# Two transformer blocks on one core: memory attention interleaved with its query projections, squared-relu fronts reordered, first value chunks 512 columns wide

## The reference

```python
def memory_cross_attention(h, mem_n, w_q, w_kv, w_o):       # first block, both layers
    q = (h @ w_q).reshape(B_, S_, MEM_HEADS, MEM_HEAD_DIM)   # 4 heads of 256
    kv = (mem_n @ w_kv).reshape(B_, M, 2, MEM_HEADS, MEM_HEAD_DIM)
    s = jnp.einsum('bshd,bmhd->bhsm', q, kv[:, :, 0]).astype(jnp.float32) * MEM_HEAD_DIM ** -0.5
    p = jax.nn.softmax(s, axis=-1).astype(h.dtype)
    o = jnp.einsum('bhsm,bmhd->bshd', p, kv[:, :, 1]).reshape(B_, S_, D_MODEL)
    return o @ w_o

def squared_relu_mlp(h, w1, w2):                             # first block, both layers; 4096 hidden
    a = jax.nn.relu(h @ w1)
    return (a * a) @ w2

# first block, layer 1: band attention; second block, layer 0: stick-breaking attention
qkv = (h @ w_qkv).reshape(B_, S_, 3, ATT_HEADS, ATT_HEAD_DIM)   # 16 heads of 64
```

## Time and profile before

| | |
|---|---|
| median of three runs | 1807.8 us |
| the profiled execution | 1808.25 us |
| its span on the core | 1806.3 us |
| TensorE busy | 1772.4 us, 98% |
| VectorE busy | 1160.9 us, 64% |
| ScalarE busy | 868.8 us, 48% |
| GpSimd busy | 62.1 us, 3% |
| HBM traffic | 318.08 MB, mean 176 GB/s |

### The profile page before, as it was taken

One profiled execution on the slowest core, in us unless ns is written; L12 is line 12 of the kernel. 1 busy time (PEld: TensorE's weight loads), 2 busy tenths in 40 slices (PEclk: granted clock), 3 DMA queues, 4 the chain that ended last, 5 costly groups with the idle time before them and its releaser, 6 DMA issues.

```text
span 1806.3 us, 25833 instructions
## 1 busy us (share of the span) xinstructions
PE 1772.4 (98%) x10482; PEld 1547.4 (86%) x10482; DVE 1160.9 (64%) x1166; ACT 868.8 (48%) x1060; POOL 62.1 (3%) x102
## 2 busy tenths in 40 slices
PE   9999999999999999999999999999999999999998
PEld 7889988888988878888888899888888888788887
DVE  6665465557456465556666755667676666876665
ACT  7535455556455454555433466533353334553343
POOL 1000000000120000000000100000000000110000
PEclk9999999999999999999999999999999999999999
DMA  9526356556546345554556553565555555336552
GB/s 310 183 70 221 106 187 202 194 186 189 164 160 229 105 162 202 197 196 155 184 189 205 169 163 117 176 208 178 194 175 186 193 194 186 118 117 210 187 184 93
DMA packets 217157, 318.08 MB, mean 176 GB/s; under 512 B 5585, under 2 KB 179809, under 8 KB 217074
## 3 DMA queue, kind: packets, MB, share of 16 engines
q1 hardware_dynamic: 212274, 300.96, 50.2%
q0 software_dynamic: 4800, 15.94, 2.8%
HBM read 315.83 MB, written 1.05 MB: 175 GB/s over the span
## 4 chain that ended last, share of the span: by engine, by line
PE 93%; DVE 4%; ACT 2%; issue 0%; DMA 0%; SPq 0%; ACTq 0%; DVEq 0%
PE Y L1824 29%; PE C L1747 22%; PE C L1751 12%; PE Y L1780 9%; PE C L1780 5%; PE C L1792 4%; PE Y L1714 3%; DVE xn L1178 1%; DVE w_lo L1137 1%; ACT xn L669 1%; PE C L2023 1%; PE C L1996 1%; PE C L1878 1%; PE Y L2043 1%; PE C L2317 1%; PE C L2035 1%
## 5 line engine op out<-in xcount | busy, mean ns | idle before, releaser
L1137 DVE TENSOR_TENSOR w_lo<-raw,w_hi 128x2048 fp32r<-128x2048 f32 x282 | 645.7, 2291 | 321.0 <-ACT w_hi L654 320.5
L654 ACT ACTIVATE w_hi<-raw 128x2048 fp32r<-128x2048 f32 x282 | 538.2, 1910 | 247.2 <-PE Y L1824 163.9
L1747 PE MATMUL C<-at_hl,w_hi 128*128 128x512 f32 x1440 | 342.8, 390 | 0.0
L1747 PEld LDWEIGHTS C<-at_hl,w_hi 128*128 128x128 f32 x1440 | 267.9, 188 | 54.1
L1824 PE MATMUL Y<-w_hi,hid_h 128*128 128x512 f32 x696 | 216.7, 392 | 0.0
L1824 PE MATMUL Y<-w_lo,hid_h 128*128 128x512 f32 x696 | 215.0, 390 | 0.0
L1824 PE MATMUL Y<-w_hi,hid_l 128*128 128x512 f32 x696 | 214.6, 390 | 0.0
L1751 PEld LDWEIGHTS C<-at_hl,w_lo 128*128 128x128 f32 x1440 | 184.9, 191 | 7.2
L1751 PE MATMUL C<-at_hl,w_lo 128*128 128x256 f32 x1440 | 187.1, 283 | 0.0
L1824 PEld LDWEIGHTS Y<-w_lo,hid_h 128*128 128x128 f32 x696 | 130.7, 188 | 28.1
L1824 PEld LDWEIGHTS Y<-w_hi,hid_l 128*128 128x128 f32 x696 | 130.7, 188 | 27.9
(11 more groups left out here) (297 smaller groups left out, 2251.9 us busy)
## 6 DMA issues: line engine op xcount, KB each, us to landing
raw<-in_ffn_w_in SPq DMA_DIRECT2D x88, 1024.0 KB, 5.1
raw<-in_w_ff SPq DMA_DIRECT2D x64, 1024.0 KB, 5.6
raw<-in_ffn_w_out SPq DMA_DIRECT2D x44, 1024.0 KB, 4.9
raw<-in_w_mem_kv SPq DMA_DIRECT2D x16, 1024.0 KB, 5.7
raw<-in_w_qkv SPq DMA_DIRECT2D x12, 1024.0 KB, 5.5
raw<-in_sb_w_qkv SPq DMA_DIRECT2D x12, 1024.0 KB, 5.2
raw<-in_w_in_ab SPq DMA_DIRECT2D x8, 1024.0 KB, 9.8
raw<-in_w_mem_q SPq DMA_DIRECT2D x8, 1024.0 KB, 5.2
```

Of the source, the lines that this page charges most:

```text
L654: nc.scalar.activation(w_hi[:, n % RING, :], raw[:, n % RAW, :], ACT.Copy).then_inc(hi_split, 1)
L1137: V.tensor_tensor(w_lo[:, n % RING, :], raw[:, n % RAW, :], w_hi[:, n % RING, :].bitcast(f32), ALU.subtract).then_inc(lo_split, 1)
L1747: mm(tiles(C[:, 2 * pair + i, :], 2), wh[:, k, i * P:(i + 1) * P], hl[:, k, :, :], start=k == 0, stop=False)
```

## The change

**Memory attention.** The stages `cols` and `softmax` become one stage `mem_att`. The scores move to banks Y2 and Y3 (`mem_bank`). TensorE computes head 0's scores behind query chunk 1 and head 1's behind chunk 2; ScalarE and VectorE have their parts of heads 0 and 1 between the roundings of chunks.

The diff, cut to its core:

```diff
-PARTS = ("v0", "q0", "k0", "q1", "k1", "q2", "k2", "v1", "q3", "k3", "v2", "v3")
-SCORES_BEHIND = {3: 0, 4: 1, 5: 2, 6: 3, 7: 4, 8: 5, 10: 6, 11: 7}
+PARTS = ("v0", "v1", "q0", "k0", "q1", "k1", "q2", "k2", "q3", "k3", "v2", "v3")
+SCORES_BEHIND = {4: 0, 5: 1, 6: 2, 7: 3, 8: 4, 9: 5, 10: 6, 11: 7}
...
@@ VectorE, meanwhile (n == 2: the one ahead of the relu front of layer 0 and of the band layer)
                 for i in range(n):
+                    if n == 2 and i == 1:
+                        norm_lo("at", then, Y)
                     lo(at.chunk + i + AHEAD)
                     if i == 0:
                         norm_scale("at", then)
-                    if i == n - 1:
+                    if n > 2 and i == n - 1:
                         norm_lo("at", then, Y)
...
@@ VectorE, mem_att
+                lo(n + 2)
+                lo(n + 3)
+                mem_max(0)
+                lo(n + 4)
+                mem_shares(0)
+                mem_max(1)
+                lo(n + 5)
+                mem_shares(1)
+                mem_max(2)
+                mem_max(3)
+                mem_shares(2)
+                mem_shares(3)
+                for i in range(4):
+                    contexts(i, at, "mem")
...
@@ ScalarE, mem_att
+                hi(n + 4)
+                mem_exps(0)
+                copied(2, specs, to, at)
+                hi(n + 5)
+                mem_exps(1)
+                copied(3, specs, to, at)
+                mem_out(0)
+                mem_out(1)
+                mem_exps(2)
+                mem_exps(3)
+                contexts(0, at, "mem")
+                mem_out(2)
...
@@ TensorE
+            def wide_front(n, at, banks, turn):
...
+                for i, j in ((0, 0), (0, 1), (1, 0), (0, 2), (1, 2)):
+                    part(i, 0, j)
+                if turn:
+                    turn_block(1, at.xn, C)
+                part(1, 0, 1)
+                for i, j in ((0, 0), (0, 1), (1, 0), (1, 1)):
+                    part(i, 1, j)
+                for i in range(2):
+                    part(i, 1, 2).then_inc(chunk_done, 1)
...
-                front_one(n, front_bank(same), at, Y if same else C, not same)
-                pair_chunk(n + 1, at_hl, 1, some=[0])
-                front_turn(at)
-                pair_chunk(n + 1, at_hl, 1, some=[1])
+                if same:
+                    for b in range(TB):
+                        last = front_part(n, at_h, at_l, b, front_bank, split, range(3))
+                    last.then_inc(chunk_done, 1)
+                    pair_chunk(n + 1, at_hl, 1, some=[0])
+                    front_turn(at)
+                    pair_chunk(n + 1, at_hl, 1, some=[1])
+                else:
+                    front_part(n, at_h, at_l, 0, front_bank, split, range(3))
+                    pair_block(n + 1, at_hl, 1, 0)
+                    turn_block(1, at.xn, Y)
+                    front_part(n, at_h, at_l, 1, front_bank, split, range(3)).then_inc(chunk_done, 1)
+                    pair_block(n + 1, at_hl, 1, 1)
+                    front_turn(at)
+                    pair_lo(n + 1, at_hl, 1).then_inc(chunk_done, 1)
```

More of the change, by code:

```diff
@@ L399, in counts @@
                 return dict(x=2)
-            if s[0] == "cols":
-                return dict(chunk=len(s[1]), copied=len(s[1]))
+            if s[0] == "mem_att":
+                return dict(chunk=4, copied=4, head=4, ctx=4)
             if s[0] == "even_cols":
@@ L520, in _ @@
                 elif s[0] == "att":
-                    for i, (name, l, c, _, _) in enumerate(s[2]):
-                        load(col(name, l, c), (n + i) % RAW, n + i)
+                    for i, spec in enumerate(s[2]):
+                        load(source(spec), (n + i) % RAW, n + i)
                     for r in range(4):
@@ L1753, in pair_chunk, with pair_block, pair_lo @@
                     last.then_inc(chunk_done, 1)
+            def pair_block(n, hl, pair, b):
+                w = w_hi[:, n % RING, :].rearrange("p (k c) -> p k c", k=KT)
+                pe.wait_ge(hi_split, n + 1)
+                tokens = slice(b * P, (b + 1) * P)
+                for i in range(2):
+                    for k in range(KT):
+                        mm(tiles(C[:, 2 * pair + i, :], 2)[:, :, tokens], w[:, k, i * P:(i + 1) * P], hl[:, k, :, tokens],
+                           start=b == 0 and k == 0, stop=False)
+            def pair_lo(n, hl, pair):
+                w = w_lo[:, n % RING, :].rearrange("p (k c) -> p k c", k=KT)
+                split_ready(n)
+                for i in range(2):
+                    for k in range(KT):
+                        last = mm(C[:, 2 * pair + i, S:2 * S], w[:, k, i * P:(i + 1) * P], hl[:, k, 0, :], start=False, stop=k == KT - 1)
+                return last
             def col_chunk(n, kind, h, l, bank, t=None, split=None, some=range(2)):
@@ L1794, in wide_chunk, with part @@
                 last.then_inc(chunk_done, 1)
+            def wide_front(n, at, banks, turn):
+                split = at.turned - 4
+                def part(i, b, j):
+                    wh, wl = (w[:, (n + i) % RING, :].rearrange("p (k c) -> p k c", k=4) for w in (w_hi, w_lo))
+                    if j == 1:
+                        pe.wait_ge(lo_split, n + i + 1)
+                    else:
+                        pe.wait_ge(hi_split, n + i + 1)
+                        pe.wait_ge(at_lo if j == 2 else at_hi, split + 2 * b + i + 1)
+                    for k in range(4):
+                        tokens = (slice(None), 4 * i + k, slice(b * P, (b + 1) * P))
+                        still, moving = ((at_h, wh), (at_h, wl), (at_l, wh))[j]
+                        last = mm(banks[b], still[tokens], moving[:, k, :], start=i == 0 and j == 0 and k == 0,
+                                  stop=(i, j, k) == (1, 1 if b == 0 else 2, 3))
+                    return last
+                for i, j in ((0, 0), (0, 1), (1, 0), (0, 2), (1, 2)):
[5 more added lines that the diff above has]
+                    part(i, 1, j)
+                for i in range(2):
+                    part(i, 1, 2).then_inc(chunk_done, 1)
             def col_halves(n, bank, at=None):
@@ L1851, in meanwhile @@
                 then = behind_post(at)
-                norm(then, Y, blocks=blocks)
+                norm(then, Y)
                 cols(specs, at, range(n, len(specs)))
@@ new lines, in mem_scores @@
+                def mem_scores(i):
+                    pe.wait_ge(cols_copied, at.copied + i + 1)
+                    if i >= 2:
+                        pe.wait_ge(probs_ready, h0 + i - 1)
+                    for b in range(TB):
+                        for k in range(2):
+                            last = mm(mem_bank(i)[:, b * S:(b + 1) * S], qT[:, 2 * i + k, b * P:(b + 1) * P],
+                                      mem_kT[:, 2 * i + k, :], start=k == 0, stop=k == 1)
+                    last.then_inc(scores_ready, 1)
@@ new lines, in mem_context @@
+                def mem_context(k):
+                    pe.wait_ge(probs_copied, h0 + k + 1)
+                    for half in range(2):
+                        for kb in range(2):
+                            first = k * S + half * P
+                            last = mm(ctx_bank("mem", k)[:, half * S:(half + 1) * S], vt[:, kb, first:first + P],
+                                      pT[k % 2][:, kb * S:(kb + 1) * S], start=kb == 0, stop=kb == 1)
+                    last.then_inc(probs_used, 1)
```

243 lines of the change are left out of this document (119 added, 124 removed).

## The result

The changed kernel took 1796.57 us (median of 6 runs, 1796.28 to 1797.47), the kernel before 1807.38 in the same comparison (6 runs, 1806.42 to 1808.2). The ratio is 0.9941 with a 95% interval of 0.9928 to 0.9954, a gain of 10.8 us. The forecast was 1799.4 and the range ended at 1797.4: the direction and the five places were right, the size was too small, and the time fell 0.8 us out of the range. The profiled execution took 1797.47 us with a span of 1795.6.

The account below looks back on a forecast made before the run. TensorE, busy 1772.4 of 1806.3 us (98%), was taken as the bound. Gains of 1.6 + 1.5 + 1.1 + 2.0 + 2.2 = 8.4 us took the 1807.8 us median to 1799.4, range 1797.4 to 1803.6.

Parts of the forecast that it names:

- Memory attention: Memory attention stage, both layers: scoring heads 0 and 1 between query chunks gains 0.8 us per layer, 1.6 in both.
- Relu front of layer 0: First transposes to second chunk: undivided front takes 7.5 us instead of 9.00, activations split during transposes; gain 1.5.
- Relu front of layer 1: `pair_block` replaces zeros and wait between the blocks; row chunk then waits for the hidden values' split; gain 1.1 us.
- Band layer: Band layer's start: first wide part need not await whole splits, 1.4 us, and wide chunks are shorter, 0.6; gain 2.0.
- costed at nothing: Eight pairs of both attention layers, one chunk later: same instructions issued, covered by TensorE's own work, so no cost.
- Stick-breaking layer: Its start: wide matmuls fill TensorE's 1.67 us wait before transposes, with a new 0.5 wait for `w_lo`; gain 2.2 us.
- The wide chunks' pace: Attention layers' value chunks: 48 column pairs save 0.6 us per layer by the profile rows, 0.1 by the skill's rule.
- Rival 2: Attention layers' wide fronts wait for weights, paying back 1.2 us in each layer: 1801.8 us; chance 0.09.
- Rival 3: Relu front of layer 1: `pair_block` runs at 0.216 us per matmul instead of 0.120, costing 3.1: 1802.5 us; chance 0.05.
- Rival 4: Attention layers: the pairs' loop through VectorE and ScalarE outlasts TensorE's step, slower than before, 1818.0 us if fully paid; chance 0.03.
- Rival 5: Whole kernel: the change does nothing because each place's wait only moves to the next norm, 1807 us; chance 0.03.

Follow-up runs that it names:

- the three with a part alone: The kernel before with only merged memory attention (1804.58 us), only the relu fronts (1804.46 us), or only the attention layers' wide fronts and tables (1802.90 us).
- the version with both small waits gone: The changed kernel with VectorE taking head 2's shares before head 3's maximum and ScalarE copying hidden values before the next rounding; 1795.52 us, ratio 0.9937.

## Why the prediction was right in its places and wrong in its size

**Memory attention: the step that failed.** The prediction had "Two more switches between column chunks and fp32 work cost 2 x 0.19 = 0.4", a "wait of 0.3" and 1.5 us lost before: 0.8 per layer, where 1.54 came. Three sizes were off. The switches cost 0 net (one group in place of two left the stage at 38.60): 0.4 of the 0.74 missing. The wait was 0.20 with its slow restart: 0.1. The remaining 0.24 is the loss before, 1.7 and not 1.5; most of it stood in the contexts of heads 2 and 3 (TensorE's timeline of the kernel before):

```profile
620.32 3.62 PE L2013 MATMUL C<-arena 128*128 128x256 f32 x16
```

From there to the row chunk it is 623.59 - 620.32 = 3.27, not 2 x 1.73 = 3.46: the group ahead of the row chunk takes 1.54 as well, so the content is 15.4 and 1.7 us were lost. One oversight lies behind the first and the third: a fp32 group's length from start to start depends on what follows it, and each price had been read with one kind of successor. This row was there to be read. The forecast's mechanism (fourth chunk followed by transposes, head 3's maximum in front of head 2's products) was as the trace shows, and the kernel with head 2's shares first showed its second half.

**Relu front of layer 0**: 1.51 of 1.5. The prediction had counted on VectorE splitting the activations first; that it matters is refuted: with the old order the front took 7.50.

**Relu front of layer 1**: 1.42 of 1.1. The cover by `pair_block` was full, the transposes came 6.60 us behind those of block 0 (before 6.47, forecast 0.2 later), and the row chunk waited for VectorE's split. The size is off by 0.3, in small pieces. The rounding began 12.29 us behind the transposes of block 0 (654.07 - 641.78), where the forecast had 661.5 - 649.05 = 12.45. From its start to the split's end it took 657.17 - 654.07 = 3.10, less than the 3.19 of the three durations: the copy starts at 655.88, 0.09 ahead of the end shown for the rounding. And the row chunk followed after 0.06. The slower row chunk gave 0.12 back.

**Band layer**: 2.27 of 2.0. The front gave 2.00 (14.68 to 12.68, transposes and both value chunks). That it is the term to the digit is chance: the wait gave 1.49 where 1.4 stood, the wide chunks 0.51 (11.52 to 11.01 by the starts) where 0.6 stood. The further 0.27 was costed at nothing. The chunks tell where part of it lies: before, eight column chunks stood behind a group of fp32 matmuls or transposes and took 5.92 each, now seven do, and here the groups of scores take 0.86 whether a chunk or transposes follow, so one such place less does save 0.16. Why the tail does not cancel here as in memory attention, no run shows; the other 0.1 is spread over the undisturbed chunks and the contexts.

**Stick-breaking layer**: 2.23 of 2.2, but not by the term as it was worked out: its front gave 2.04. Transposes without a wait and 0.42 for `w_lo` in place of 0.5, as forecast; the 28 matmuls behind took 6.46 instead of 6.36, the first ones after a wait being slower, and the first transposes' own wait of 0.8 stayed. The prediction had also taken q0's start from the chain of waits (1034.02), while the timeline, from which v0's start came, has the first matmul of q0 at 1033.86; that alone is 0.16 too much. The other 0.19 of the layer came where nothing was forecast, as in the band layer: one column chunk less stands behind a group (5.89 against 5.76).

**The wide chunks' pace.** By the isolated gap in the section Back-to-back issue gap of the Trainium skill's "TensorE: Matmul & The Clock Gate" wide chunks would save 0.1 per layer; the section itself keeps that formula apart from streams of weight loads and matmuls, as these are. The trace does not agree with 0.1: by the starts 48 wide matmuls took 11.01 where two column chunks take 11.52, a saving of 0.5, near the 0.6 of the sum.

**The rivals.** Rival 2 (the wide fronts wait for weights): 0.42 in the stick-breaking layer, which the sum held already, nothing in the band layer. Rival 3 (`pair_block` slow): refuted, 0.120 per matmul in both blocks. The prediction's row against it was the duration of a bf16 matmul, not a pace, and could not have settled it. The warning on non-contiguous access patterns in "PSUM — Partial Sum Buffer", Specifications (TRN2), of the Trainium skill is not borne out for two pieces of 128 columns. Rival 4 (the pairs' loop): no wait in eight chunks in a row, in either layer. Rival 5: the norm's waits were shorter by 2.3 us and most of the gain lay elsewhere.

**The range.** Two things put the time below it. The first is the size of the sum: 8.4 where the code's own gain, with the start-up left out, is 10.3, of which memory attention holds 1.5 of the 1.9. That gain alone would just have been inside, for the range ended at 1807.8 - 1797.4 = 10.4. The second has nothing to do with the change: the medians differ by 10.8, and the kernel before took 1807.38 in this comparison, 0.4 less than the 1807.8 from which the forecast was counted. Both lie within the 2.2 us by which the start-up varies, and no term stood for it; on which side of the range's end the median fell was luck. In its own terms the range was too tight as well: memory attention gave 1.54 per layer over a bound of 1.5, the band layer 2.27 over 2.1, and the bounds were treated as independent while one misreading pushed two layers the same way.

## What to carry to other kernels

Read a group's cost from start to start on both sides of a boundary, with each kind of successor, before a price is put on a switch; a tail that is counted once on each side makes a move look dear that is free. Fill a wait with real work that is due anyway, and then look which engine's strict order brings the next input: here two swaps of independent instructions on VectorE and ScalarE gave another 0.8 us. With effects under 2 us, compare from a landmark behind the first loads to the end, and not device times.

## What was not expected of the hardware

**The start varies, and what follows hardly does.** With the same code and data up to there, the first query chunk began at 180.37, 179.97, 180.12, 178.45, 179.59, 178.91, 178.89, 179.39, 180.61 and 178.54 us in ten profiled executions, a spread of 2.2 us. In the two compared first, the whole difference was there at 25 us: the first wide chunk started at 24.92 and 24.58, and 155.45 and 155.39 us lay between it and the query chunk. In the three with a part alone it was 155.47, 155.42 and 155.48. From there on kernels whose stages are alike agreed within about 0.1 us over 1600.

Two differences in the traces go with it. ScalarE's first instruction on x, which waits for the load of x, began at 4.78 to 5.67 us. And TensorE's eight transposes of the second token block took 1.91 us in four executions and 1.03 to 1.66 in the others, with no wait shown ahead of them. TensorE's timelines, first of the kernel before, then of the version with both small waits gone:

```profile
11.56 1.91 PE L1878 MATMUL C<-ident,xn 128*128 128x128 f32 x8
```

```profile
11.00 1.03 PE L1966 MATMUL C<-ident,xn 128*128 128x128 f32 x8
```

From ScalarE's first instruction on x to the first wide chunk it is 18.3 us in the two executions where these transposes took 1.03 and 1.04, 18.5 to 19.1 in the four where they took 1.10 to 1.66, and 19.6 to 19.9 in the four where they took 1.91: the slower the transposes, the later the rest begins. The granted clock reads 1.00 from 6 to 24 us in all ten, so the traces do not say why TensorE's pace differs. The device times of the kernel before spread as much (1806.2 to 1808.4 in 26 runs); that each run's time follows its start-up was seen in profiled executions only.

**A matmul after a wait is slower.** Four transposes took 0.49 us after a wait of 0.14, else 0.43, and a row chunk of 24 matmuls 5.59 after a wait of 0.3, else 5.47. In the kernel before, the scores of head 2 took 1.83 behind a wait, else 1.73. A short wait thus cost 0.06 to 0.12 more than its own length in these three places.
